# Half norms of a two-layer diffusion trunk: scale and shift move from VectorE to ScalarE, VectorE works in larger passes

## The chip, the core and the metric

The kernel runs on one core of a Trainium2 chip. The metric is the device time of one execution in microseconds; three runs of the kernel before gave a median of 2887.71 us (2882.85 to 2890.86). Engines are called PE (the matrix engine, TensorE), PEld (its weight loads), DVE (VectorE), ACT (ScalarE), POOL (GpSimd) and SP (the queue that starts the weight DMAs).

## The reference, cut to what matters

Two streams, 256 latent tokens (x) and 256 context tokens (h), go through two layers of the same shape: a half-step SwiGLU block, three token mixers side by side with gates, a second SwiGLU block. Each sub-layer is wrapped in RMS norms, and each norm ahead of a sub-layer is followed by an adaptive scale and shift:

```python
def rms_norm(x, g):
    xf = x.astype(jnp.float32)
    y = xf * lax.rsqrt(jnp.mean(xf * xf, axis=-1, keepdims=True) + EPS)
    return (y * g.astype(jnp.float32)).astype(x.dtype)

def modulate(x, shift, scale):
    return x * (1 + scale) + shift

def ffn_sublayer(t, shift, scale, gate, g_pre, g_post, w_in, w_out):
    y = swiglu(modulate(rms_norm(t, g_pre), shift, scale), w_in, w_out)
    return t + FFN_RES * gate * rms_norm(y, g_post)
```

All arithmetic is float32. D_MODEL is 1024, the FFN's inner width 2816.

## The kernel before, in words

**Layout.** Activations lie transposed: the 1024 channels are 8 chunks of 128 partitions, and the free axis holds the tokens, 256 latent ones and then 256 context ones. `x`, `work`, `xhi` and `xlo` are 128 x 8 x 512 tiles. A scale or a shift is one number for each channel and stream, so for one chunk and one stream it is a column of 128 numbers (`mods`); the inverse root `inv` is one number for each token, the same in all partitions and chunks.

**Products in three parts.** PE multiplies in a reduced format, so both operands are split in a high part and the rest. For a group of weights (128 x 1024, 512 KB, loaded into `raw`) ACT makes the high part `whi` (L1166) and DVE the rest `wlo` (L1474). PE then runs the group's first part, high and low activations by `whi` (L1934 and L1935, or L1998 and L2000 for products whose output is turned), and its second part, high activations by `wlo` (L1942, or L1995). There are two buffers of `whi` and `wlo`: the split of group k can begin only when PE has used group k-2, and group k's first part waits for `whi`, its second part for `wlo`. The activations' split is `xhi` and `xlo`; a first group waits for `xlo` chunk by chunk.

**Half norms.** In eight places the norm between two sub-layers is done for the 256 tokens of one stream alone, while PE multiplies for the other stream. Each engine runs such a norm as a generator that is advanced once for each group of the products beside it (`beside`): in slot k an engine first does its work for the products (the split of group k, and perhaps an output tile, L1279 and L1282), then the k-th piece of the norm. Pieces that find no group left follow one after another. Each engine works strictly in the order written. The products beside the eight norms are: the second stream's FFN output (12 groups; three norms, near 409, 1676 and 2050 us), values of the mixers (10 groups; two norms, near 444 and 2085 us), the mixers' output projection (8 groups, an output tile in each slot; one norm, near 1303 us) and the first groups of the next FFN for one stream (8 groups; two norms, near 1334 and 1710 us).

**The pieces of one half norm.** DVE: slot 1 refines the inverse root of the branch's output (Newton steps, L617, L630, L631 and L621); slots 2 and 3 add the residual in two batches of four chunks (L1651, L1654); slots 3 and 4 sum squares (L1661, L1682), which ACT made (L1323); slot 5 refines the second inverse root; slots 6 to 9 compute x times scale times inverse root, two chunks in each (`scaled`, L1633); slots 7 to 10 compute the low parts, two chunks in each (`normed_low`, L1643, which adds the shift once more and subtracts `xhi`). ACT: slot 5 makes the inverse root; slot 6 is empty; slots 7 to 10 add the shift and round to `xhi`, two chunks in each (`normed_high`, L1330). POOL adds the squares of the output tiles into `acc` (L1028).

Of the kernel before, what the change touches and what calls it, by code (L numbers as in the profile page):

```python
# [8 lines left out]
F32 = mybir.dt.float32  # L9
F32R = mybir.dt.float32r  # L10
ALU = mybir.AluOpType
ACT = mybir.ActivationFunctionType
AX_X = mybir.AxisListType.X

P = 128
D = 1024
KC = D // P
S = 256
# [27 lines left out]
BATCHES = 2  # L46
# [109 lines left out]
def make_plan():  # L156
# [14 lines left out]

    def half_norm(layer, post, pre, half):

        adds = {"stat": 2, "inv": 2, "gated": BATCHES, "x": BATCHES, "xsq": BATCHES, "xsum": 3, "scaled": KC,
                "xhi": KC, "xlo": KC}
        return add("norm", layer, post=post, pre=pre, tokens=S, span=(half * S, half * S + S), adds=adds, half=True)

    def last_products(layer, post, pre, **kw):
# [147 lines left out]
def build(nc, io, silu_rows, x_kept, out):  # L326
# [3 lines left out]
    with ExitStack() as ctx:  # L330
# [103 lines left out]
        def sem(name):  # L434
# [19 lines left out]
        first_shift = sem("first_shift")  # L454
        ada_dot = sem("ada_dot")
        done = {name: sem(f"{name}_done") for name in (
            "ghi", "glo", "gated", "xsq", "xsum", "sq", "acc", "stat", "inv", "x", "scaled", "xhi",
            "xlo", "rope", "m", "mhi", "mlo", "vk", "lsq", "lstat", "lln", "linv", "lvar", "lt", "lhi", "llo",
            "score", "bias", "exp", "prob", "turned", "pt", "pv", "yraw", "ysq", "yln", "yinv", "yfactor",
            "yscaled", "yturned", "yback", "yhi", "ylo", "ybhi", "yblo", "ln", "refined", "made")}  # L460
# [33 lines left out]
        def base(ph, name):  # L494
            return ph.at.get(name, 0)
# [5 lines left out]
        def batch(t, ph, b):  # L501

            return t[:, b * KC // BATCHES:(b + 1) * KC // BATCHES, ph.span]
# [119 lines left out]
        def newton(step, dve, count, bank_, cols, width):  # L623

            dst, v = inv[:, cols], tmp[:, 0, cols]
            newton_start(dve, count, bank_, cols, width, v)
            dve.wait_ge(done["refined"], count)

            dve.wait_ge(done["inv"], count)
            step(dve.tensor_tensor(v, v, dst, ALU.mult))  # L630
            step(dve.tensor_tensor(v, v, dst, ALU.mult))  # L631
            newton_end(step, dve, dst, v)
# [518 lines left out]
        def _(act):  # L1151
# [173 lines left out]
            def normed_high(ph, c):  # L1325

                l, sub = ph.pre
                act.wait_ge(done["scaled"], base(ph, "scaled") + c + 1)
                for s in streams(ph.span):
                    last = act.activation(xhi[:, c, sl(s)], work[:, c, sl(s)], ACT.Identity,  # L1330
                                          bias=mods[:, l, 3 * sub, c, s:s + 1])
                last.then_inc(done["xhi"], 1)

            def act_norm(ph):

                inverse(HALF_STAT, ph.span, D, base(ph, "stat") + 1)
                yield
                yield
                square(ph, 0)
                yield  # L1340
                square(ph, 1)
                yield
                inverse(HALF_STAT, ph.span, D, base(ph, "stat") + 2)
                yield
                yield
                for c in range(0, KC, 2):
                    normed_high(ph, c)
                    normed_high(ph, c + 1)
                    yield

            use_table(SILU)
# [114 lines left out]
        def _(dve):  # L1466
# [162 lines left out]
            def scaled(ph, c):  # L1629

                l, sub = ph.pre
                for s in streams(ph.span):
                    last = dve.scalar_tensor_tensor(work[:, c, sl(s)], x[:, c, sl(s)],  # L1633
                                                    mods[:, l, 3 * sub + 1, c, s:s + 1], inv[:, sl(s)],
                                                    ALU.mult, ALU.mult)
                last.then_inc(done["scaled"], 1)
# [11 lines left out]
            def residual_added(ph, b):  # L1648
# [5 lines left out]
                dve.tensor_tensor(batch(x, ph, b), batch(x, ph, b), batch(work, ph, b), ALU.add)\  # L1654
                   .then_inc(done["x"], 1)

            def squares_summed(ph, b):

                dve.wait_ge(done["xsq"], base(ph, "xsq") + b + 1)
                first, second = squares[:, 4 * b:4 * b + 2, :], squares[:, 4 * b + 2:4 * b + 4, :]  # L1660
                dve.tensor_tensor(first, first, second, ALU.add).then_inc(done["xsum"], 1)  # L1661
# [8 lines left out]
            def dve_norm(ph):  # L1670

                newton(step, dve, base(ph, "inv") + 1, HALF_STAT, ph.span, D)
                residual_ready(ph)
                yield
                residual_added(ph, 0)
                yield
                residual_added(ph, 1)
                squares_summed(ph, 0)
                yield
                squares_summed(ph, 1)  # L1680
                dve.wait_ge(done["xsum"], base(ph, "xsum") + 2)
                dve.tensor_tensor(squares[:, 0:2, :], squares[:, 0:2, :], squares[:, 4:6, :],  # L1682
                                  ALU.add).then_inc(done["xsum"], 1)
                yield
                newton(step, dve, base(ph, "inv") + 2, HALF_STAT, ph.span, D)
                yield
                for c in range(0, KC + 2, 2):
                    if c < KC:
                        scaled(ph, c)
                        scaled(ph, c + 1)  # L1690
                    if c:
                        normed_low(ph, c - 2)
                        normed_low(ph, c - 1)
                    yield

            spreads = 0

# [482 lines left out]
```

## Time and profile before

| | |
|---|---|
| median of three runs | 2887.71 us |
| the profiled execution's own time | 2884.27 us |
| its span, first to last instruction | 2882.2 us |
| PE busy | 2770.0 us, 96% |
| DVE busy | 1743.8 us, 61% |
| ACT busy | 1250.8 us, 43% |
| POOL busy | 249.1 us, 9% |
| granted TensorE clock, mean | 0.985 of full |

Busy times are unions over the span. A timeline row gives start and duration in us, engine, line, operation, output and inputs, shapes and how many instructions were merged; a bracket is idle time of the engine before it and what ended it. Consecutive instructions of DVE and of ACT overlap by some 0.1 us at their ends, so the pace is read from start to start.

### The profile page before, as it was taken

How to read it: one execution, taken by the hardware profiler on the slowest of the kernel's cores; microseconds unless marked ns; L12 is line 12 of the kernel's file. 1: busy time of each engine (PE TensorE's matmuls, PEld its weight loads, DVE VectorE, ACT ScalarE, POOL GpSimd, SP SyncE). 2: the span in 40 equal slices, each digit the busy share in tenths (PEclk: the TensorE clock that was granted, in tenths of full speed). 3: DMA queues.
4: the chain of work that ended last, by engine and by line, in shares of the span. 5: the costliest groups of instructions: out<-in, count | busy, mean ns of one | idle time of the engine just before them, and what ended most of it. 6: DMA issues, size and time to landing. Idle time of an engine off the chain costs nothing.

```text
span 2882.2 us, 42837 instructions
## 1 busy us (share of the span) xinstructions
PE 2770.0 (96%) x15754; PEld 2301.8 (80%) x15754; DVE 1743.8 (61%) x2907; ACT 1250.8 (43%) x2227; POOL 249.1 (9%) x342
## 2 busy tenths in 40 slices
PE   6999999999889999999999999999999899998997
PEld 4888898876656676788888898888988677878997
DVE  5677366656745444358676386773778765635764
ACT  2232355336545434445322363223553655555443
POOL 0010010111200000011000000000102120001000
PEclk8999999999999999999999999999999999999999
DMA  5555357331111121145455355553565221424654
GB/s 224 181 188 197 108 156 241 126 101 37 45 37 38 52 77 66 44 146 175 160 191 171 114 175 177 201 182 97 176 198 186 69 66 59 137 66 154 227 175 130
DMA packets 106643, 385.48 MB, mean 134 GB/s; under 512 B 12289, under 2 KB 14081, under 8 KB 104193
## 3 DMA queue, kind: packets, MB, share of 16 engines
q1 hardware_dynamic: 86370, 303.82, 32.6%
q0 software_dynamic: 20128, 79.70, 8.4%
q8 instruction: 94, 1.54, 0.2%
q14 instruction: 51, 0.42, 0.0%
HBM read 379.27 MB, written 4.20 MB: 133 GB/s over the span
## 4 chain that ended last, share of the span: by engine, by line
PE 85%; DVE 9%; ACT 2%; issue 2%; DMA 1%; POOL 0%; SPq 0%; DVEq 0%; POOLq 0%; ACTq 0%
PE ps L1934 23%; PE ps L1935 22%; PE ps L1942 22%; PE ps L879 3%; PE ps L917 3%; PE ps L896 3%; DVE wlo L1474 2%; PE ps L1998 1%; PE ps L2000 1%; PE ps L1995 1%; PE ps L869 1%; DVE mx L767 1%; PE ps L875 1%; DVE work L1633 1%; ACT prob L683 1%
## 5 line engine op out<-in xcount | busy, mean ns | idle before, releaser
L1474 DVE TENSOR_TENSOR wlo<-raw,whi 128x1024 fp32r<-128x1024 f32 x572 | 696.2, 1225 | 442.2 <-ACT whi L1166 441.4
L1934 PE MATMUL ps<-xhi,whi 128*128 128x512 f32 (+1 forms) x2432 | 827.2, 354 | 16.5 <-DVE xlo L1643 16.5
L1935 PE MATMUL ps<-xlo,whi 128*128 128x512 f32 (+1 forms) x2432 | 818.3, 351 | 0.0
L1166 ACT ACTIVATE whi<-raw 128x1024 fp32r<-128x1024 f32 x572 | 604.8, 1057 | 483.6 <-PE ps L1942 443.9
L1934 PEld LDWEIGHTS ps<-xhi,whi 128*128 128x128 f32 x2432 | 465.8, 192 | 85.8 <-DVE xlo L1643 18.8
L1935 PEld LDWEIGHTS ps<-xlo,whi 128*128 128x128 f32 x2432 | 466.7, 192 | 57.0
L1942 PE MATMUL ps<-xhi,wlo 128*128 128x512 f32 (+1 forms) x2432 | 507.4, 351 | 1.4 <-DVE wlo L1474 1.4
L1942 PEld LDWEIGHTS ps<-xhi,wlo 128*128 128x128 f32 x2432 | 401.8, 191 | 59.3 <-DVE wlo L1474 2.0
L1710 DVE SCALAR_TENSOR_TENSOR work<-ada,work 128x1024 f32<-128x1024 f32 x256 | 299.8, 1221 | 4.4 <-DMA ada<-in_ada_rows 4.4
L1934 PE MATMUL ps<-ghi,whi 128*128 128x256 f32 (+1 forms) x968 | 279.5, 314 | 1.9 <-ACT whi L1166 1.9
L1935 PE MATMUL ps<-glo,whi 128*128 128x256 f32 (+1 forms) x968 | 278.6, 314 | 0.0
L767 DVE TENSOR_REDUCE mx<-ps 128x2 f32<-128x1024 f32 (+1 forms) x120 | 125.2, 1045 | 241.3 <-PE ps L883 88.1
L1408 ACT ACTIVATE ghi<-tmp 128x512 f32 (+2 forms) x88 | 51.0, 580 | 343.0 <-DVE tmp L1793 343.0
L1934 PEld LDWEIGHTS ps<-ghi,whi 128*128 128x128 f32 x968 | 183.2, 189 | 15.2 <-issue 2.8
L1935 PEld LDWEIGHTS ps<-glo,whi 128*128 128x128 f32 x968 | 183.0, 189 | 12.1
L1942 PE MATMUL ps<-ghi,wlo 128*128 128x256 f32 (+1 forms) x968 | 168.4, 314 | 3.4 <-DVE wlo L1474 3.4
L1793 DVE TENSOR_TENSOR tmp<-tmp,ps 128x512 f32<-128x512 f32 (+1 forms) x88 | 54.6, 621 | 181.4 <-PE ps L1942 181.4
L1942 PEld LDWEIGHTS ps<-ghi,wlo 128*128 128x128 f32 x968 | 140.9, 188 | 16.2 <-DVE wlo L1474 4.1
L896 PE MATMUL ps<-ident,prob 128*128 128x128 f32 x640 | 107.0, 282 | 32.3 <-ACT ya L729 14.1
L896 PEld LDWEIGHTS ps<-ident,prob 128*128 128x128 f32 x640 | 72.4, 142 | 65.0 <-issue 32.1
L1048 POOL DMA_DIRECT2D ada<-in_ada_rows x128 | 68.6, 536 | 607.4 <-DVE work L1710 603.8
L683 ACT ACTIVATE prob<-ps,mx 128x512 f32<-128x512 f32 (+1 forms) x144 | 87.3, 612 | 76.6 <-DVE mx L767 73.5
(209 smaller groups left out, 3374.4 us busy)
## 6 DMA issues: line engine op xcount, KB each, us to landing
raw<-in_ffn_in SPq DMA_DIRECT2D x192, 512.0 KB, 4.8
ada<-in_ada_rows POOLq DMA_DIRECT2D x128, 512.0 KB, 4.4
raw<-in_merge SPq DMA_DIRECT2D x96, 512.0 KB, 3.7
raw<-in_ffn_out SPq DMA_DIRECT2D x88, 512.0 KB, 3.6
raw<-in_ffn_out SPq DMA_DIRECT2D x44, 384.0 KB, 3.2
raw<-in_v_a SPq DMA_DIRECT2D x32, 512.0 KB, 4.3
raw<-in_qk_a SPq DMA_DIRECT2D x32, 512.0 KB, 3.6
raw<-in_wo SPq DMA_DIRECT2D x24, 512.0 KB, 3.7
```

The source lines that it names most:

```text
L683: last = act.activation(prob(u)[:, n, 0:nk], ps[:, SCORE + 2 * e + n, 0:nk], ACT.Exp, bias=shift[:, e, n:n + 1], accum_out=sm[:, r, n:n + 1])
L767: largest = dve.tensor_reduce(mx[:, e, :], ps[:, SCORE + 2 * e:SCORE + 2 * e + 2, 0:nk], AX_X, ALU.max, negate=True)
L879: last = pe.matmul(o, q[half, b, cols], k[half, kb, ks], start=True, stop=not masked)
L896: last = pe.transpose(ps[:, TURN, cs], prob(u)[:, n, cs], ident[:, :])
L917: last = pe.matmul(ps[rows, OUT, to:to + P], a, w, start=kc == kc0, stop=kc == T // P - 1)
L1048: pool.dma_start(ada[:, slot, :], src).then_inc(ada_loaded[slot], 16)
L1166: act.activation(whi[:, g.ring(SPLIT), :], raw[:, g.ring(RAW), :], ACT.Copy).then_inc(hi_ready, 1)
L1474: dve.tensor_tensor(wlo[:, g.ring(SPLIT), :], raw[:, g.ring(RAW), :], whi[:, g.ring(SPLIT), :].bitcast(F32), ALU.subtract).then_inc(lo_rea ...
L1710: dve.scalar_tensor_tensor(products[:, s, :], ada[:, slot, :], 1.0, c_all[:, s * D:(s + 1) * D], ALU.mult, ALU.mult, accum_out=to).then_in ...
L1934: pe.matmul(o, w, hi[:, first + c, ph.span], start=start, stop=False)
L1935: pe.matmul(o, w, lo[:, first + c, ph.span], start=False, stop=False)
L1942: last = pe.matmul(ps[:, n.ring(BANKS), ph.span], wlo[:, s, col:col + P], hi[:, first + c, ph.span], start=False, stop=stop)
```

## The change

The generator pieces of the half norms change, on ACT and DVE alone. DVE multiplies x by the inverse root in two passes of four chunks (`normalized`, in slots 5 and 6); ACT applies scale and shift to each chunk in place (`modulated`) and rounds two chunks at once to `xhi` (`highs`), in slots 6, 7 and 8, the last with four chunks; DVE subtracts two chunks at once (`lows`), in slots 7, 8 and, twice, 9. A new counter, `modulated`, stands between ACT's two steps. The norms of full width are as before.

```diff
+            def modulated(ph, c):
+
+                l, sub = ph.pre
+                s = ph.span.start // S
+                act.wait_ge(done["scaled"], base(ph, "scaled") + c * BATCHES // KC + 1)
+                act.activation(work[:, c, ph.span], work[:, c, ph.span], ACT.Identity,
+                               bias=mods[:, l, 3 * sub, c, s:s + 1], scale=mods[:, l, 3 * sub + 1, c, s:s + 1])\
+                   .then_inc(done["modulated"], 1)
+
+            def highs(ph, c):
+
+                act.wait_ge(done["modulated"], base(ph, "modulated") + c + 2)
+                act.activation(xhi[:, c:c + 2, ph.span], work[:, c:c + 2, ph.span], ACT.Copy)\
+                   .then_inc(done["xhi"], 2)
+
...
                 inverse(HALF_STAT, ph.span, D, base(ph, "stat") + 2)
                 yield
-                yield
-                for c in range(0, KC, 2):
-                    normed_high(ph, c)
-                    normed_high(ph, c + 1)
+                for chunks in (range(2), range(2, 4), range(4, KC)):
+                    for c in chunks:
+                        modulated(ph, c)
+                        if c % 2:
+                            highs(ph, c - 1)
                     yield
...
+            def normalized(ph, b):
+
+                many = [P, KC // BATCHES, S]
+                dve.tensor_tensor(batch(work, ph, b), batch(x, ph, b),
+                                  inv[:, ph.span].unsqueeze(1).to_broadcast(many), ALU.mult).then_inc(done["scaled"], 1)
+
+            def lows(ph, c):
+
+                dve.wait_ge(done["xhi"], base(ph, "xhi") + c + 2)
+                dve.tensor_tensor(xlo[:, c:c + 2, ph.span], work[:, c:c + 2, ph.span],
+                                  xhi[:, c:c + 2, ph.span].bitcast(F32), ALU.subtract).then_inc(done["xlo"], 2)
+
...
                 newton(step, dve, base(ph, "inv") + 2, HALF_STAT, ph.span, D)
-                yield
-                for c in range(0, KC + 2, 2):
-                    if c < KC:
-                        scaled(ph, c)
-                        scaled(ph, c + 1)
-                    if c:
-                        normed_low(ph, c - 2)
-                        normed_low(ph, c - 1)
-                    yield
+                normalized(ph, 0)
+                yield
+                normalized(ph, 1)
+                yield
+                lows(ph, 0)
+                yield
+                lows(ph, 2)
+                yield
+                lows(ph, 4)
+                lows(ph, 6)
```

## Rows read from the trace of the kernel before

**Rows 1.** The page: busy time by engine, and shares of the chain by engine.

```profile
PE 2770.0 (96%) x15754; PEld 2301.8 (80%) x15754; DVE 1743.8 (61%) x2907; ACT 1250.8 (43%) x2227; POOL 249.1 (9%) x342
PE 85%; DVE 9%; ACT 2%; issue 2%; DMA 1%; POOL 0%; SPq 0%; DVEq 0%; POOLq 0%; ACTq 0%
```

**Rows 2.** One line's instructions: durations min/median/max in ns, first and last start.

```profile
L1651 DVE TENSOR_TENSOR work<-work,inv x16: 1210/1218/1759, 406.4 to 2085.9; 128x1024 f32<-128x1024 f32 x16
```

**Rows 3.** Timeline of PE, the norm near 409 us: part starts, groups 6 to 9.

```profile
421.29 1.12 PE L1942 MATMUL ps<-ghi,wlo 128*128 128x256 f32 x8
422.25 0.29 PE L1934 MATMUL ps<-ghi,whi 128*128 128x256 f32 x1
...
425.13 0.29 PE L1934 MATMUL ps<-ghi,whi 128*128 128x256 f32 x1
...
427.29 0.29 PE L1934 MATMUL ps<-ghi,whi 128*128 128x256 f32 x1
```

**Rows 4.** Timeline of DVE, the same norm, from the end of its refinement.

```profile
419.23 0.42 DVE L621 SCALAR_TENSOR_TENSOR inv<-tmp,inv 128x256 f32<-128x256 f32 x1
419.69 1.23 DVE L1474 TENSOR_TENSOR wlo<-raw,whi 128x1024 fp32r<-128x1024 f32 x1
420.84 1.36 DVE L1633 SCALAR_TENSOR_TENSOR work<-x,mods,inv 128x256 f32<-128x256 f32 x2
...
423.26 0.87 DVE L1633 SCALAR_TENSOR_TENSOR work<-x,mods,inv 128x256 f32<-128x256 f32 x2
```

**Rows 5.** Timeline of ACT, the same norm.

```profile
419.49 1.06 ACT L1166 ACTIVATE whi<-raw 128x1024 fp32r<-128x1024 f32 x1 [0.33 <-PE ps L1942]
420.45 0.37 ACT L1279 ACTIVATE tmp<-ps 128x256 f32<-128x256 f32 x1
420.72 0.47 ACT L1282 ACTIVATE work<-ps,mods 128x256 f32<-128x256 f32 x1
...
423.77 0.91 ACT L1330 ACTIVATE xhi<-work,mods 128x256 fp32r<-128x256 f32 x2
```

**Rows 6.** Timelines near 1361 us: ACT and DVE on a 128x512 tile.

```profile
1361.41 0.63 ACT L1408 ACTIVATE ghi<-tmp 128x512 fp32r<-128x512 f32 x1 [2.27 <-DVE tmp L1793]
...
1362.07 0.69 DVE L1799 TENSOR_TENSOR glo<-tmp,ghi 128x512 fp32r<-128x512 f32 x1 [0.70 <-ACT ghi L1408]
```

**Rows 7.** Timelines, norms near 444, 1303, 1334 us: split of group 6, PE's second part.

```profile
454.05 1.22 DVE L1474 TENSOR_TENSOR wlo<-raw,whi 128x1024 fp32r<-128x1024 f32 x1
455.99 1.07 PE L1995 MATMUL ps<-wlo,xhi 128*128 128x512 f32 x4
1313.90 0.74 POOL L1028 TENSOR_TENSOR acc<-acc,tmp 128x256 f32<-128x256 f32 x1 [3.99 <-ACT tmp L1279]
1314.09 1.64 DVE L1474 TENSOR_TENSOR wlo<-raw,whi 128x1024 fp32r<-128x1024 f32 x1
1316.28 1.12 PE L1942 MATMUL ps<-mhi,wlo 128*128 128x256 f32 x8
1345.08 1.23 DVE L1474 TENSOR_TENSOR wlo<-raw,whi 128x1024 fp32r<-128x1024 f32 x1
1346.92 1.12 PE L1942 MATMUL ps<-xhi,wlo 128*128 128x256 f32 x8
```

**Rows 8.** Waits of PE near 1310:1330, 1340:1358 and 1716:1733 us: total, times, longest.

```profile
PE ps L1934 <- DVE xlo L1643: 2.8, 2, 2.3
...
PE ps L1934 <- DVE xlo L1643: 1.5, 2, 0.8
...
PE ps L1934 <- DVE xlo L1643: 1.1, 2, 0.7
```

**Rows 9.** Windows: length, busy of PE, PEld, DVE, ACT, POOL; clock, DMA, GB/s.

```profile
1320.00:1332.00 12.00, 9.16 (x48) 8.38 (x47) 10.07 (x19) 5.46 (x10) 1.20 (x1) 0.72 0.35 117
1352.00:1360.00 8.00, 7.12 (x41) 6.62 (x42) 5.36 (x10) 5.08 (x7) 1.61 (x3) 0.79 0.62 222
1727.00:1731.00 4.00, 2.86 (x16) 2.06 (x15) 3.49 (x9) 3.30 (x6) 0.21 (x1) 1.00 0.46 138
```

More of the change, by code:

```diff
@@ L172, in half_norm @@
     def half_norm(layer, post, pre, half):
-        adds = {"stat": 2, "inv": 2, "gated": BATCHES, "x": BATCHES, "xsq": BATCHES, "xsum": 3, "scaled": KC,
-                "xhi": KC, "xlo": KC}
+        adds = {"stat": 2, "inv": 2, "gated": BATCHES, "x": BATCHES, "xsq": BATCHES, "xsum": 3,
+                "scaled": BATCHES, "modulated": KC, "xhi": KC, "xlo": KC}
         return add("norm", layer, post=post, pre=pre, tokens=S, span=(half * S, half * S + S), adds=adds, half=True)
@@ L456, in build @@
         done = {name: sem(f"{name}_done") for name in (
-            "ghi", "glo", "gated", "xsq", "xsum", "sq", "acc", "stat", "inv", "x", "scaled", "xhi",
+            "ghi", "glo", "gated", "xsq", "xsum", "sq", "acc", "stat", "inv", "x", "scaled", "modulated", "xhi",
             "xlo", "rope", "m", "mhi", "mlo", "vk", "lsq", "lstat", "lln", "linv", "lvar", "lt", "lhi", "llo",
```

## The prediction, made before the changed kernel ran

> **What bounds the kernel now.** I read the page first. PE is busy 96% of the span and has 85% of the chain that ended last; DVE has 9%, ACT 2% [rows 1]. So a microsecond that PE stands still is a microsecond of the whole, and work taken from DVE or ACT is worth only the waits of PE that it ends. The page's 61% and 43% for DVE and ACT are averages over stages and say nothing of a half norm. The residual is multiplied in two passes for each half norm and 16 times in all, so there are eight half norms [rows 2]. Then I read PE's waits around each of the eight. After the second inverse root PE waits on the norm's result in three of them alone: 2.8 us near 1323, 1.5 us near 1352, 1.1 us near 1728, 5.4 us in sum [rows 8]. These are the norms with 8 groups beside them, where slots 9 and 10 find no group. Around the first two the granted clock is below full, 0.72 on average over 12 us and 0.79 over 8 us, around the third it is 1.00 [rows 9]. PE was busy nearly all of the time at the lower level, 1.2 in place of 2.4 GHz, so the shares missing, 12 x 0.28 and 8 x 0.21, are the price: 3.4 and 1.7 us. In the other five norms PE has no wait from there on. So the change can win at most 5.4 + 5.1 = 10.5 us; what it can lose is read from the slack of the weight splits in slots 6 to 9.
>
> **The pieces and their prices.** DVE loses eight `scaled` and eight `normed_low` (a pair takes 0.87 us, 0.79 until the next can start, since DVE's instructions overlap by 0.08 [rows 4]), 6.3 us; it gains two `normalized`, nearest row the four-chunk multiply by the same broadcast, 1.22 us, 1.15 from start to start, up to 1.76 [rows 2, 4], and four `lows`, 0.69 us, nearest row the 128x512 subtraction [rows 6], 0.6 from start to start: 4.7 us. DVE does 1.6 us less, but earlier: a whole `normalized` now stands ahead of the split of group 6.
>
> ACT loses eight `normed_high`, two of which take 0.91 us (0.82 from start to start). It gains eight `modulated`, which no row shows. With a column as scale and one as shift, the nearest rows are 0.47 us (scale only, 128x256) and half of the pair of 0.91 (shift only) [rows 5]; bounds 0.37 us, the bare square of such a tile, and 0.6 us, the 128x512 copy. I take 0.41 from start to start. And it gains four `highs`, 0.63 us, 0.54 from start to start with ACT's overlap of 0.1 [rows 5, 6], each of which must wait until the second `modulated` has written (0.50 + 0.03 in place of 0.41). A pair of chunks costs 0.41 + 0.53 + 0.54 = 1.48 us instead of 0.82; a norm 2.6 us more. Nobody hides that by ACT's 57% idle: ACT's next act in each slot is a weight split that PE needs within one group's 2.88 us.
>
> **One FFN-output norm, slot by slot** (near 409, 1676, 2050 us). DVE's refinement ends at 419.65. `normalized` 0 takes 419.69 to 420.92, and the split of group 6 starts at 420.84 instead of 419.69 [rows 4], ending at 422.06. PE wanted it at 421.29 [rows 3]: wait 0.81 us, first part of group 7 due at 423.06 instead of 422.25.
> ACT in slot 6, empty before, now waits in order for `normalized` 0: `modulated` 420.95 and 421.36, `highs` 421.89, and only then the high split of group 7 at 422.43, which began at 419.49 before [rows 5]. It ends at 423.47: wait 0.46 us.
> From there ACT has no pause: split 0.97, output tile 0.68 (the starts at 419.49, 420.45 and the end of the tile's pair in rows 5), chunks 2 and 3 1.48, and the split of group 8 starts at 425.56, ends at 426.60; PE is due at 423.52 + 2.88 = 426.40: wait 0.25.
> Slot 8 holds four chunks, 2.96 us: split of group 9 starts at 426.53 + 2.96 = 429.49, ends at 430.53. Group 8 is the short third part of a tile (422.25 to 425.13 is a long group, 425.13 to 427.29 a short one of 2.16 [rows 3]), so PE is due at 426.65 + 2.16 = 428.81: wait 1.77. Then ACT has nothing more of the norm and catches up.
> Sum 3.3 us for each, 9.9 us for three. Nothing given back: these norms had no wait after slot 5.
>
> **Two value norms** (near 444, 2085 us), the same steps. The split of group 6 moves from 454.05 to 455.20, ends 456.42, PE wanted it at 455.99 [rows 7]: 0.48. The high split of group 7, by the same chain, 0.55. In slot 7 ACT carries two value tiles (0.95 us) instead of an output tile: 0.68. Slot 8: 1.2. Sum 2.9, twice 5.8 us.
>
> **The output-projection norm** (near 1303 us). The split of group 6 already took 1.64 us beside a POOL addition [rows 7]; now `normalized` takes that place and its stretch, and the split ends near 1316.9, PE wanted it at 1316.28: 0.6. Then 0.5 and 0.25 as above, the tile in each slot. Next comes the first group of the following product, which waits on `xlo`: chunks 2, 4 and 6 arrive behind ACT's slot 8 at 1323.3, 1324.3 and 1325.8, the last half microsecond of matmuls then ending at 1326.3. Before, without the half clock, that group would have ended near 1326.1, by its last `xlo`. With one more stretch by POOL +1.0 is the far end, +0.2 the near one; I take +0.6.
>
> One rule of the Trainium skill weighs on this. In the output-projection norm a DVE instruction with two operands in SBUF ran 1.64 us beside a POOL addition, 1.23 alone [rows 4, 7]. "SBUF — State Buffer", section "Who interferes with whom", says that a DVE instruction with two SBUF inputs contends with a GpSimd instruction that reads SBUF; by it `normalized` and `lows` are no safer than what they replace, and the trace agrees. A stretch of 0.4 us in each of the four norms with output tiles would make the sum 1.6 us longer.
>
> **The two norms beside the next FFN** (near 1334, 1710 us) have no output tiles. The split of group 6: 1345.08 + 1.15 + 1.22 = 1347.45 against 1346.92 [rows 7], 0.5 (0.24 in the other); then 0.45; ACT, without tiles, is in time for group 8; chunk 2 of the first following group waits 0.95, chunk 4 0.1, chunk 6 0.75, 2.5 to 2.8 us in all, against 2.3 us by which that group was stretched before. +0.3 each, 0.6 in all. The freed slot buys nothing here: what was late behind DVE's slot 10 is now late behind ACT's slot 8.
>
> **Sum:** 9.9 + 5.8 + 0.6 + 0.6 = 16.9 us. The clock I leave as it was: waits of the same size end in the same places. The profiled execution took 2884.27 us, 3.4 less than the median of the three runs; the mean of all four executions is 2886.4. 2886.4 + 16.9 = 2903.
>
> **The rivals.**
> *ACT's idle hides it (faster).* Place: ACT's slots 6 to 8. If ACT's passes were at their low bound and the chain through `normalized` 0 cost nothing, DVE's lighter slots would end the waits of rows 8 and the half clock behind them: 10.5 us less, 2876. It decides from the point where the high split of group 7 ends before 422.2. For it: DVE is full in slots 6 to 9 (2.72 us of work in slots of 2.88), ACT idle 43% to 57%. Against: ACT's in-order wait for `normalized` 0, which ends at 420.92 and leaves 0.3 us for 2.5 us of work. 8%. The Trainium skill's "Perfetto Trace Analysis", section "Optimizing Scalar/DVE Operations", speaks for this rival: with DVE saturated, moving work to Scalar may help, and larger operations raise throughput; by that rule the time would be 2876. The same section says that where the engines cause bubbles elsewhere, smaller instructions finish sooner, which is my case.
> *It cancels (within 0.3%).* Only the first two waits of each norm stand: 3 x 1.27 + 2 x 1.03 + 1.1 + 1.0 + 0.7 = 8.7 us, and a half-clock stretch or two goes (5.1), or ACT's low bound empties the waits of slot 8: +0 to +8, 2886 to 2894. 24%.
> *The clock falls at the new waits.* A new wait of 1.8 us stands in three norms and of 1.2 in two; if each brings a stretch at 1.2 GHz that costs 1.7 us, as the one near 1352 did, it is five times 1.7, 8.5 us more: 2912. For it: the clock fell around waits of this size. Against: around 1.1 us in two pieces it stayed full [rows 8, 9]. 10%.
>
> **Chances.** Forecast, 2896.5 to 2909: 58%. Rivals 8, 24 and 10%. Slower by over 0.3% (8.7 us, about what a measurement of this kernel can tell from no change) is 68%, within 0.3% 24%, faster 8%. The forecast's own range is 2896.5 to 2909; for 8 in 10 it reaches down into the cancelling case and up into the clock case: 2885 to 2914.
>
> **What would show it.** In the changed profile: PE waits on `wlo` (L1474) for group 6 in all eight norms, 0.2 to 0.9 us; PE waits on `whi` (L1166) for groups 7 to 9, together 2.5 us in FFN-output norms; ACT without a pause between slots 6 and 9; `modulated` at 0.5 us, `normalized` at 1.2. I am wrong if PE has no such waits, if the waits on `xlo` vanish in the three norms with 8 groups, or if ACT's pair of chunks takes under 1.1 us.

## The result and the profile after

The changed kernel takes 2905.21 us in the median of five runs (2903.29 to 2911.32), beside 2887.71 for five runs of the kernel before (2882.74 to 2890.86): a ratio of 1.0064, 95% interval 1.0047 to 1.0081. It is slower, by more than the 0.3% that the prediction counts as no change. The forecast was 2903, within 2885 to 2914.

The page after, busy times by engine and the chain by engine (they answer to [rows 1]):

```profile
span 2901.6 us, 42845 instructions
...
PE 2770.0 (95%) x15754; PEld 2296.6 (79%) x15754; DVE 1733.4 (60%) x2827; ACT 1272.4 (44%) x2259; POOL 253.3 (9%) x342
...
PE 82%; DVE 9%; ACT 5%; issue 2%; DMA 1%; POOL 1%; SPq 0%; DVEq 0%; ACTq 0%; POOLq 0%
```

PE does the same work in the same busy time and stands still for longer; ACT's share of the chain rose from 2% to 5%, though it is busy for only 22 us more. PE's waits over the whole program, largest first (engine and line, who ended the wait: us in total, times, longest):

```profile
PE ps L1963 <- ACT whi L1166: 11.3, 11, 2.0
...
PE ps L1971 <- DVE wlo L1490: 9.2, 10, 1.1
...
PE ps L1963 <- DVE xlo L1682: 5.6, 6, 1.0
...
PE ps L2027 <- ACT whi L1166: 4.8, 6, 1.3
```

L1963 and L2027 are the first parts of a group (L1934 and L1998 before), L1971 the second part (L1942), L1682 the new `lows`. For `whi` PE waited 2.5 us in the kernel before, none of it in a half norm; now it is 11.3 + 4.8 = 16.1. The row of before:

```profile
PE ps L1934 <- ACT whi L1166: 2.5, 3, 1.9
```

The first FFN-output norm, near 409 us. PE's timeline of the kernel before at the start of this stretch, second part of group 5:

```profile
418.52 0.87 PE L1942 MATMUL ps<-ghi,wlo 128*128 128x256 f32 x6
```

and of the kernel after, the same part and the part starts of [rows 3]:

```profile
417.20 0.87 PE L1971 MATMUL ps<-ghi,wlo 128*128 128x256 f32 x6
...
420.78 1.21 PE L1971 MATMUL ps<-ghi,wlo 128*128 128x256 f32 x8 [0.65 <-DVE wlo L1490]
...
422.53 0.36 PE L1963 MATMUL ps<-ghi,whi 128*128 128x256 f32 x1 [0.54 <-ACT whi L1166]
...
425.72 0.39 PE L1963 MATMUL ps<-ghi,whi 128*128 128x256 f32 x1
...
430.17 0.36 PE L1963 MATMUL ps<-ghi,whi 128*128 128x256 f32 x1 [2.04 <-ACT whi L1166]
```

The stretch begins 1.32 us earlier than before. Second part of group 6: 0.51 earlier, so 0.81 lost. First part of group 7: 0.28 later, 1.60 lost. Group 8: 0.59 later, 1.91 lost. Group 9: 2.88 later, 4.20 lost. DVE and ACT over the same stretch (they answer to [rows 4, 5]):

```profile
417.90 0.43 DVE L621 SCALAR_TENSOR_TENSOR inv<-tmp,inv 128x256 f32<-128x256 f32 x1
418.36 1.23 DVE L1676 TENSOR_TENSOR work<-x,inv 128x1024 f32<-128x1024 f32 x1
419.51 1.22 DVE L1490 TENSOR_TENSOR wlo<-raw,whi 128x1024 fp32r<-128x1024 f32 x1
420.64 1.22 DVE L1676 TENSOR_TENSOR work<-x,inv 128x1024 f32<-128x1024 f32 x1
422.42 1.23 DVE L1490 TENSOR_TENSOR wlo<-raw,whi 128x1024 fp32r<-128x1024 f32 x1 [0.56 <-ACT whi L1166]
423.56 1.23 DVE L1682 TENSOR_TENSOR xlo<-work,xhi 128x512 fp32r<-128x512 f32 x1
```

```profile
419.62 1.09 ACT L1339 ACTIVATE work<-work,mods 128x256 f32<-128x256 f32 x2 [1.79 <-DVE work L1676]
420.81 0.63 ACT L1346 ACTIVATE xhi<-work 128x512 fp32r<-128x512 f32 x1
421.35 1.04 ACT L1166 ACTIVATE whi<-raw 128x1024 fp32r<-128x1024 f32 x1
422.29 0.36 ACT L1279 ACTIVATE tmp<-ps 128x256 f32<-128x256 f32 x1
422.56 0.47 ACT L1282 ACTIVATE work<-ps,mods 128x256 f32<-128x256 f32 x1
422.91 1.08 ACT L1339 ACTIVATE work<-work,mods 128x256 f32<-128x256 f32 x2
424.09 0.63 ACT L1346 ACTIVATE xhi<-work 128x512 fp32r<-128x512 f32 x1
424.63 1.04 ACT L1166 ACTIVATE whi<-raw 128x1024 fp32r<-128x1024 f32 x1
425.57 1.08 ACT L1339 ACTIVATE work<-work,mods 128x256 f32<-128x256 f32 x2
426.75 0.63 ACT L1346 ACTIVATE xhi<-work 128x512 fp32r<-128x512 f32 x1
427.29 1.07 ACT L1339 ACTIVATE work<-work,mods 128x256 f32<-128x256 f32 x2
428.45 0.63 ACT L1346 ACTIVATE xhi<-work 128x512 fp32r<-128x512 f32 x1
428.99 1.99 ACT L1166 ACTIVATE whi<-raw 128x1024 fp32r<-128x1024 f32 x2
```

What the reader is to see: ACT sits idle for 1.79 us in front of its first new instruction, with the high split of group 7 behind it in the queue; and from 419.62 it has no pause longer than 0.1 us until the two splits at 428.99, which it makes back to back because both are due by then. ACT is 44% busy over the program and busy all but 0.4 us of these 11.

I measured all eight norms like this, by the starts of PE's second part of one and the same group in both traces: the first just ahead of the norm's second half, the other where the waits have ended. Clock parts come from the share of time at 1.2 GHz.

| norm (near, us, in the kernel before) | foretold | measured step | of it clock | without clock |
|---|---|---|---|---|
| 409, FFN output | 3.3 | 4.2 | 0 | 4.2 |
| 444, values | 2.9 | 3.9 | 0 | 3.9 |
| 1303, projection | 0.6 | 0.5 | -1.7 | 2.2 |
| 1334, next FFN | 0.3 | 0.1 | -1.7 | 1.8 |
| 1676, FFN output | 3.3 | 5.7 | +1.7 | 4.0 |
| 1710, next FFN | 0.3 | 1.3 | 0 | 1.3 |
| 2050, FFN output | 3.3 | 6.1 | +1.7 | 4.4 |
| 2085, values | 2.9 | 3.9 | 0 | 3.9 |
| sum | 16.9 | 25.7 | 0 | 25.7 |

The rest of the program gave back 6.3 us in this one execution: 1.3 ahead of the first norm and 5.1 in the last layer's attention and FFN, whose code did not change. The clock column rests on these windows of the kernel after (columns as in [rows 9], to which the first two answer):

```profile
1330.00:1342.00 12.00, 10.01 (x65) 9.29 (x64) 8.92 (x11) 7.17 (x12) 1.60 (x2) 0.86 0.40 121
1359.00:1367.00 8.00, 6.18 (x47) 5.52 (x46) 5.24 (x6) 7.13 (x11) 1.61 (x3) 1.00 0.63 217
1703.00:1712.00 9.00, 6.96 (x46) 6.79 (x46) 4.70 (x5) 5.01 (x8) 1.16 (x1) 0.81 0.52 158
2086.00:2095.00 9.00, 7.56 (x51) 7.59 (x52) 5.33 (x5) 3.94 (x6) 1.15 (x1) 0.81 0.45 157
```

The projection norm's stretch at the lower clock is half as long as before (12 x 0.14 = 1.7 us lost, not 3.4), that of the norm behind it is gone (before 1.7), and two have come after FFN-output norms (9 x 0.19 = 1.7 each). Over the eight norms the sum is zero.

### The profile page after: what moved, and what is told of

Read it like the earlier page. It is cut to its first block, busy times and chain, and to the rows that moved or that the text cites. A ratio compares the mean times of both kernels' runs of the same rounds, so it can differ in the third digit from the quotient of the medians.

```text
span 2901.6 us, 42845 instructions
## 1 busy us (share of the span) xinstructions
PE 2770.0 (95%) x15754; PEld 2296.6 (79%) x15754; DVE 1733.4 (60%) x2827; ACT 1272.4 (44%) x2259; POOL 253.3 (9%) x342
## 4 chain that ended last, share of the span: by engine, by line
PE 82%; DVE 9%; ACT 5%; issue 2%; DMA 1%; POOL 1%; SPq 0%; DVEq 0%; ACTq 0%; POOLq 0%
PE ps L1963 22%; PE ps L1964 22%; PE ps L1971 22%; PE ps L917 3%; PE ps L879 3%; PE ps L896 2%; DVE wlo L1490 2%; ACT whi L1166 1%; PE ps L869 1%; PE ps L2027 1%; PE ps L2029 1%; PE ps L2024 1%; ACT work L1339 1%; DVE mx L767 1%; PE ps L875 1%
## 5 line engine op out<-in xcount | busy, mean ns | idle before, releaser
L1963 PE MATMUL ps<-xhi,whi 128*128 128x512 f32 (+1 forms) x2432 | 824.3, 353 | 17.8 <-DVE xlo L1659 11.0
L1963 PEld LDWEIGHTS ps<-xhi,whi 128*128 128x128 f32 x2432 | 464.0, 191 | 87.2 <-DVE xlo L1659 12.0
L1971 PE MATMUL ps<-xhi,wlo 128*128 128x512 f32 (+1 forms) x2432 | 507.0, 351 | 2.1 <-DVE wlo L1490 2.0
L1971 PEld LDWEIGHTS ps<-xhi,wlo 128*128 128x128 f32 x2432 | 400.9, 191 | 60.8 <-DVE wlo L1490 3.1
L1963 PE MATMUL ps<-ghi,whi 128*128 128x256 f32 (+1 forms) x968 | 281.0, 315 | 9.8 <-ACT whi L1166 9.6
L1963 PEld LDWEIGHTS ps<-ghi,whi 128*128 128x128 f32 x968 | 183.8, 190 | 24.8 <-issue 11.6
L1971 PE MATMUL ps<-ghi,wlo 128*128 128x256 f32 (+1 forms) x968 | 169.2, 315 | 5.7 <-DVE wlo L1490 5.7
L1971 PEld LDWEIGHTS ps<-ghi,wlo 128*128 128x128 f32 x968 | 141.8, 190 | 19.2 <-DVE wlo L1490 7.0
L1028 POOL TENSOR_TENSOR acc<-acc,tmp 128x256 f32<-128x256 f32 (+1 forms) x68 | 68.9, 1014 | 612.6 <-ACT tmp L1279 452.5
```

Source lines behind the costliest of these rows:

```text
L1028: pool.tensor_tensor(acc[:, cols], acc[:, cols], tmp[:, number, cols], ALU.add)\
L1963: pe.matmul(o, w, hi[:, first + c, ph.span], start=start, stop=False)
L1971: last = pe.matmul(ps[:, n.ring(BANKS), ph.span], wlo[:, s, col:col + P], hi[:, first + c, ph.span], start=False, stop=stop)
```

## The experiments

Theory A: a queue worked in order is late for PE's next group for two reasons, DVE's large pass ahead of group 6's low split, and ACT's new work ahead of the high splits of groups 7 to 9 (where it stands, and how long it takes). Rivals: ACT's load alone (B), group 6's delay as the root of all (C), the slot with four chunks alone (D), placement alone (E). The experiments were compared with two sets of 29 runs of the kernel before, with medians of 2885.01 (first four experiments) and 2885.32 us (last four); the changed kernel's ratio is that to its five runs. "Norms" is the sum of the eight steps in the profiled execution, measured as above, "rest" what the remainder of the program differs by.

The last three columns take the clock apart. A run with a mean granted clock c over a span T has lost about (1 - c) x T to the lower clock, as the prediction reckons it from [rows 9]; in the kernel before that is 43.5 and 44.5 us on average. "Norms, no clock" leaves this out of the eight steps by the stretches at 1.2 GHz in each trace, an estimate: 1.7 us for a stretch of 3.4. "Runs, clock" is the difference of that loss between the mean of all timed runs and the mean of the 29, "runs, no clock" the difference of the mean times that is left, known to 1 to 2 us.

| kernel | median us | ratio, 95% interval | norms | rest | norms, no clock | runs, clock | runs, no clock |
|---|---|---|---|---|---|---|---|
| changed kernel | 2905.21 | 1.0064 (1.0047 to 1.0081) | +25.7 | -6.3 | +25.7 | -7 | +27 |
| ACT one slot later | 2891.62 | 1.0021 (1.0011 to 1.0032) | +7.1 | +3.1 | +8.8 | -1.6 | +7.2 |
| last slot split | 2901.10 | 1.0050 (1.0033 to 1.0066) | +15.1 | +1.1 | +18.5 | -4.3 | +18.9 |
| all one slot later | 2890.71 | 1.0011 (0.9999 to 1.0023) | +9.0 | +7.2 | +3.9 | -0.6 | +5.0 |
| old pieces, new slots | 2882.84 | 0.9997 (0.9984 to 1.0010) | +4.4 | -4.2 | +7.8 | -9.6 | +9.1 |
| two-chunk passes | 2903.07 | 1.0056 (1.0041 to 1.0070) | +18.5 | +5.0 | +21.9 | -4.4 | +22.1 |
| no rounding pass | 2886.73 | 1.0000 (0.9992 to 1.0009) | -0.4 | -2.6 | +3.0 | -2.3 | +2.7 |
| new pieces in short norms | 2889.49 | 1.0012 (1.0003 to 1.0021) | +2.2 | -6.0 | +5.6 | -3.1 | +6.0 |
| mixed chunks | 2881.40 | 0.9982 (0.9973 to 0.9991) | -3.5 | +4.5 | -0.1 | -4.0 | -0.6 |

Without the clock the profiled norms and the timed runs agree within 2 us for all nine kernels: what the change does to the waits is in both, and what the clock adds or gives back is separate from it.

**ACT one slot later.** The same instructions, ACT's slot 6 empty again and its last four chunks in two slots.

```diff
                 inverse(HALF_STAT, ph.span, D, base(ph, "stat") + 2)
                 yield
-                for chunks in (range(2), range(2, 4), range(4, KC)):
+                yield
+                for chunks in (range(2), range(2, 4), range(4, 6), range(6, KC)):
...
                 lows(ph, 4)
+                yield
                 lows(ph, 6)
```

> The changed kernel with ACT's pieces where they stood before: slot 6 empty, two chunks in each of slots 7 to 10, and DVE's four subtractions in slots 7, 8, 9 and 10; DVE's two large passes stay in slots 5 and 6. Theory A (ACT's place: it waits in order for DVE's first pass ahead of the high split of group 7, and slot 8 holds four chunks): PE's waits on the high split go in the five norms with 10 and 12 groups (some 2.6 us in each of three, 2.4 in each of two, 12.7 us), PE's waits for group 6's low split stay (3.5 us in all eight), the three norms with 8 groups gain about 1 us at most: 2890 to 2893 us. Rival B (ACT's load: its passes cost 3 us more per norm wherever they stand): 2902 to 2906. Rival C (everything follows from group 6's late low split): 2902 to 2906, with the waits on the high split still there.

2891.6 us. PE's waits in the first FFN-output norm, all that is left there (416 to 436 us):

```profile
PE ps L1973 <- DVE wlo L1491: 0.7, 1, 0.7
```

There is not one wait on a high split in the five long norms (those with 10 and 12 groups beside them), with ACT's load unchanged. That fells rival B (load wherever it stands) and rival C (group 6 as the root): group 6 is as late as in the changed kernel and nothing follows from it. 13.6 us of the 20 lost are ACT's place, its early start and its last slot with four chunks together; with the clock taken off it is 20 of 27. What remains is the waits for group 6, in the five long norms and the projection norm, and the three short norms (those with 8 groups).

**Last slot split.** ACT starts in slot 6 as in the changed kernel, but has two chunks in slot 8 and two in slot 9.

```diff
-                for chunks in (range(2), range(2, 4), range(4, KC)):
+                for chunks in (range(2), range(2, 4), range(4, 6), range(6, KC)):
...
                 lows(ph, 4)
+                yield
                 lows(ph, 6)
```

> The changed kernel with ACT's last slot split in two: ACT in slots 6, 7, 8 and 9, two chunks each; DVE's subtractions in slots 7, 8, 9 and 10. Theory A: the wait for group 9's high split falls from 2.0 to about 0.4 us in three norms and from 1.3 to about 0 in two, 7 us; the waits for groups 6 and 7 stay: 2897 to 2900 us. Rival B (load): 2902 to 2906. Rival D (only the four chunks in one slot matter): 2890 or less, the waits for group 7 gone too.

2901.1 us, 1 us over the expected range and 4 under the changed kernel; the intervals of the two overlap, and the traces tell them apart. PE's timeline in the first FFN-output norm:

```profile
421.42 1.22 PE L1972 MATMUL ps<-ghi,wlo 128*128 128x256 f32 x8 [0.66 <-DVE wlo L1490]
423.18 0.36 PE L1964 MATMUL ps<-ghi,whi 128*128 128x256 f32 x1 [0.54 <-ACT whi L1166]
429.12 0.36 PE L1964 MATMUL ps<-ghi,whi 128*128 128x256 f32 x1 [0.34 <-ACT whi L1166]
```

Group 9's wait is 0.34 in place of 2.04, group 7's is what it was. So the slot with four chunks is 1.7 of the 4.2 us. The rest, with rival D fallen, is the early start, of DVE's pass (0.81 us) and of ACT's pieces.

**All one slot later.** DVE's two passes also move, behind the low split of group 6.

```diff
                 newton(step, dve, base(ph, "inv") + 2, HALF_STAT, ph.span, D)
+                yield
                 normalized(ph, 0)
                 yield
                 normalized(ph, 1)
-                yield
                 lows(ph, 0)
```

> As the kernel with ACT's pieces in slots 7 to 10, and DVE's two large passes one slot later as well, in slots 6 and 7, behind the low split of group 6. Theory A: no wait for group 6's low split, none on high splits but 0.3 us or so in the norms with output tiles; in the three norms with 8 groups the last chunks come 1 to 1.5 us later than in the kernel before, since ACT's pair of chunks takes 1.7 us where it took 0.8: 2888 to 2892 us, some 1 to 3 us under the kernel whose DVE passes stand in 5 and 6. Rival B (load): still over 2900.

2890.7 us. In the long norms no view lists a wait of PE; their steps are 0.3 to 0.5 us each. The three short norms pay: PE waits 3.8, 2.5 and 2.6 us for `xlo` there, where it was 2.8, 1.5 and 1.1 [rows 8], and their steps are 1.0, 2.1 and 3.6 us, of which the clock is 0, 1.7 and 3.4. The new arithmetic is all but free where groups stand beside it, and it is longer than the old one where they don't.

**Old pieces, new slots.** The kernel before, its single-chunk instructions put where the change puts its own.

```diff
                 newton(step, dve, base(ph, "inv") + 2, HALF_STAT, ph.span, D)
-                yield
-                for c in range(0, KC + 2, 2):
...
+                for c in range(4):
+                    scaled(ph, c)
+                yield
+                for c in range(4, KC):
+                    scaled(ph, c)
+                yield
+                for chunks in (range(2), range(2, 4), range(4, KC)):
+                    for c in chunks:
+                        normed_low(ph, c)
+                    yield
```

(ACT likewise: `normed_high` for chunks 0 and 1, 2 and 3, and 4 to 7 in slots 6 to 8.)

> The arithmetic of the kernel before (DVE multiplies by scale and inverse root chunk by chunk and adds the shift in the subtraction, ACT adds the shift) in the slots of the changed kernel: DVE four chunks in slot 5 and four in slot 6, subtractions 2, 2 and 4 in slots 7 to 9; ACT 2, 2 and 4 chunks in slots 6 to 8. Theory A in its two halves: the low split of group 6 is late by DVE's 1.6 us ahead of it (1.0 to 1.4 us in each of five norms), but ACT gets its first chunks after 0.5 us instead of 1.2 and four chunks take 1.6 us instead of 3.4, so no wait on a high split: 2891 to 2895 us. If the slots alone were the cause (rival E): 2902 to 2906. If the load alone were (rival B): 2887.

2882.8 us, no different from the kernel before: a miss, 8 us under the lower end of what I expected. The mechanism is there: in the first FFN-output norm PE waits 1.1 us for group 6's low split and never for a high one.

```profile
418.15 0.91 ACT L1330 ACTIVATE xhi<-work,mods 128x256 fp32r<-128x256 f32 x2 [1.05 <-DVE work L1632]
418.97 1.04 ACT L1166 ACTIVATE whi<-raw 128x1024 fp32r<-128x1024 f32 x1
...
422.77 1.69 ACT L1330 ACTIVATE xhi<-work,mods 128x256 fp32r<-128x256 f32 x4
425.02 1.06 ACT L1166 ACTIVATE whi<-raw 128x1024 fp32r<-128x1024 f32 x1 [0.56 <-PE ps L1942]
```

Four chunks take ACT 1.69 us, not 3.4, and it waits for PE again behind them. The long norms' steps are 1.1 to 1.7 us, 7.1 in sum (forecast: 1.0 to 1.4 each). I had left out what the short norms get (-1.4, -1.1 and -0.2 us, of which the clock is 1.7 in each of the first two), and the rest of the program was 4.2 us shorter in this execution. The timed runs show where the cost went: nine of the 12 had a granted clock of 0.988 to 0.990, where the kernel before has 0.985 on average. The clock gave back 9.6 us, and without it this kernel is 9.1 us slower, within the 6 to 10 that I expected. So the delays are real and the time that hid them is the clock's; why this kernel kept the higher clock longer is open. Rival E (slots alone, 2902 to 2906) is out either way: in the same slots the changed kernel lost 27 us without the clock, and the difference is its longer ACT work.

**Two-chunk passes.** The changed kernel with `normalized` over two chunks, one pass in slot 5 and three in slot 6.

```diff
-                many = [P, KC // BATCHES, S]
-                dve.tensor_tensor(batch(work, ph, b), batch(x, ph, b),
+                many = [P, 2, S]
+                dve.tensor_tensor(work[:, 2 * b:2 * b + 2, ph.span], x[:, 2 * b:2 * b + 2, ph.span],
...
-                normalized(ph, 1)
+                for b in range(1, KC // 2):
+                    normalized(ph, b)
```

> The changed kernel with DVE's multiplication by the inverse root in passes of two chunks: one in slot 5, ahead of the low split of group 6, three in slot 6. The slots of ACT stay. Theory A: what stands ahead of that split falls from 1.15 to 0.6 us, so PE's waits for group 6's low split fall from 3.5 us in all eight norms to under 1, and ACT gets its first chunk 0.54 us sooner; the wait for the high split of group 7 follows the same shift and stays near 0.5, group 9's 2.0 and 1.3 stay: some 4 us less than the changed kernel, 2899 to 2902. Rival (the first pass doesn't matter, ACT's own time does): no change, 2903 to 2906.

2903.1 us: 1 over the expected range and within the changed kernel's interval, so the timing does not tell. The trace does: group 6 is 0.3 us late in place of 0.8 to 1.2 in the FFN-output norms and no longer late in the value norms; their steps are 0.5 us shorter each where the clock is the same. ACT's waits are as before:

```profile
421.50 0.36 PE L1964 MATMUL ps<-ghi,whi 128*128 128x256 f32 x1 [0.55 <-ACT whi L1166]
429.14 0.36 PE L1964 MATMUL ps<-ghi,whi 128*128 128x256 f32 x1 [2.02 <-ACT whi L1166]
```

**No rounding pass.** ACT's pair of chunks without its second step. This kernel leaves the scale and the shift out of the low parts, so it is a measurement and no replacement; DVE's subtraction takes as long as before (684 ns).

```diff
-                act.activation(work[:, c, ph.span], work[:, c, ph.span], ACT.Identity,
+                act.activation(xhi[:, c, ph.span], work[:, c, ph.span], ACT.Identity,
                                bias=mods[:, l, 3 * sub, c, s:s + 1], scale=mods[:, l, 3 * sub + 1, c, s:s + 1])\
-                   .then_inc(done["modulated"], 1)
+                   .then_inc(done["xhi"], 1)
...
                         modulated(ph, c)
-                        if c % 2:
-                            highs(ph, c - 1)
```

> The changed kernel without ACT's second step: the scale-and-shift instruction writes xhi itself, rounded, and there is no pass of two chunks behind it; this leaves the scale and the shift out of the low part (DVE subtracts xhi from the unscaled product), which takes DVE the same time. A pair of chunks costs ACT about 1.0 us in place of 1.72, in unchanged slots. Theory A (a slot's ACT work must fit ahead of its next split): no wait for the high split of group 7, 0.3 to 0.5 us left of 2.0 for group 9, the low split of group 6 late as before, the last chunks 1 to 1.5 us sooner in the three short norms: 15 to 19 us less than the changed kernel, 2884 to 2890. Rival (placement alone, one slot too early): 2898 or more, group 7 still late by 0.5 us because ACT waits for DVE's pass.

2886.7 us, as fast as the kernel before, in the changed kernel's slots. PE in the first FFN-output norm:

```profile
419.40 1.22 PE L1969 MATMUL ps<-ghi,wlo 128*128 128x256 f32 x8 [0.66 <-DVE wlo L1488]
425.91 0.36 PE L1961 MATMUL ps<-ghi,whi 128*128 128x256 f32 x1 [0.21 <-ACT whi L1166]
```

The second step, `highs` with its wait, is what makes the slots overflow: 0.72 us for each pair, and without it 18 of the 20 us are gone (24 of 27 without the clock). With the first experiment this settles the cause as place and length together. Take either away and the waits on high splits go, but for 0.2 us in each FFN-output norm here.

**New pieces in short norms.** The change in the three norms with 8 groups alone.

```diff
                 inverse(HALF_STAT, ph.span, D, base(ph, "stat") + 2)
                 yield
+                if not short(ph):
+                    yield
+                    for c in range(0, KC, 2):
+                        normed_high(ph, c)
+                        normed_high(ph, c + 1)
+                        yield
+                    return
...
```

(DVE likewise: its pieces of the kernel before where the norm isn't short.)

> The changed kernel's pieces in the three norms with 8 groups beside them alone, the kernel before's in the other five. Theory A: the five norms are as before, the three others each 1.3 to 2.2 us longer, less or more 1.7 for each stretch at half clock that comes or goes: 2886 to 2891. If the freed slot helped anywhere, it would be here: rival, 2875 to 2882.

2889.5 us. The five long norms' steps are 0.0 us, the short ones' 0.8, 0.2 and 1.3, the first two with 1.7 us of clock given back each. The freed slot wins nothing where it was freed.

**Mixed chunks.** What the experiments point to: DVE is full in the short norms, ACT, where it has no tile, has about 1.9 us beside its split in each of slots 7 and 8 (2.88 less 0.95), one new pair's worth. So in the short norms half of the chunks go the new way, one slot later than the change has them.

```diff
+                if short(ph):
+                    normalized(ph, 0)
+                    yield
+                    for c in (4, 6):
+                        scaled(ph, c)
+                        scaled(ph, c + 1)
+                        lows(ph, c - 4)
+                        yield
+                    for c in range(4, KC):
+                        normed_low(ph, c)
+                    return
...
```

(This is DVE's part. ACT makes scale, shift and rounding of chunks 0 to 3 in slots 7 and 8, and `normed_high` of chunks 4 to 7 in slots 8 and 9.)

> The kernel before, but in the three norms with 8 groups the first four chunks go the new way (one DVE pass in slot 6, ACT's scale and shift in slots 7 and 8, two subtractions of two chunks) and the last four the old way (DVE's scale in slots 7 and 8, ACT's shift in slots 8 and 9, single subtractions). DVE, which is full there, does 0.85 us less per norm, ACT has room for its 0.9 us more per pair. Theory A: the last xlo comes 0.1 us sooner in the projection norm and 0.5 us in the two others, no new wait on a split: 2883 to 2886, which these runs can't tell from the kernel before; the trace can. Rival (ACT's passes delay the following splits here too): over 2888, with waits on high splits in the trace.

2881.4 us, a ratio of 0.9982 (0.9973 to 0.9991) to the kernel before: small, its interval under 1, the fastest of all, and 1.6 us under the expected range. PE's waits in the short norm near 1719 us:

```profile
PE ps L1993 <- DVE xlo L1702: 1.2, 1, 1.2
```

One wait of 1.2 us where there were two of 1.1 in sum, with slower matmuls behind each [rows 8]; by the starts of the parts the step is -0.3 us, not quite the expected 0.5. The steps of the two others are -1.7 and -1.5, and in both the stretch at 1.2 GHz is 3.4 us shorter, 1.7 us of time: without the clock the three steps sum to -0.1. The 11 timed runs say the same, 4.0 us of their 4.5 us gain in the mean is the clock's, and -0.6 is left, less than its own uncertainty of 1.3. So the moved work costs nothing here and by itself wins nothing that can be told from zero; what was won is clock.

## Why the prediction was right

It named the direction, the place and the mechanism. The waits it named are in the trace but for two: beside the next FFN, group 6's second part is 0.2 us late in both norms (foretold 0.5 and 0.24), and no view lists a wait there. That the time came out 2 us from the forecast is in part luck, as the point on the sum says. Step by step:

- *The low split of group 6 is late by one DVE pass.* Foretold 0.81 us of loss in the FFN-output norm, measured 0.81 (0.80 and 1.19 in the two later ones). `normalized` took 1.22 us as its nearest row. Right.
- *ACT waits in order for the first pass, group 7's high split behind it.* Foretold 0.46, measured 0.79. Right in kind; of the 0.33 missing, 0.24 is the next point, and 0.09 that PE's first matmul starts 0.14 us behind the end of the split, not 0.05.
- *A pair of chunks costs ACT 1.48 us.* It costs 1.72: `modulated` with a column for scale and one for shift took 0.59 us, near the far bound I had given it and not the row with one column that I took, and 0.5 from start to start in place of 0.41; after the wait for its write `highs` begins 0.1 us later, not 0.03. This is the mis-sized term. Slot 8 holds two pairs, so group 9's loss is 2.29 and not 1.77; over the four groups of an FFN-output norm it makes 4.2 of 3.3, over a value norm 3.9 of 2.9.
- *The projection norm.* PE's wait for group 7 was foretold as 0.5, for `whi`; it is 1.12, and it is a wait for an output tile:

```profile
1323.83 1.22 PE L1971 MATMUL ps<-mhi,wlo 128*128 128x256 f32 x8 [0.51 <-DVE wlo L1490]
1326.17 0.36 PE L1963 MATMUL ps<-mhi,whi 128*128 128x256 f32 x1 [1.12 <-ACT work L1282]
...
1331.17 0.39 PE L1963 MATMUL ps<-xhi,whi 128*128 128x256 f32 x1 [1.03 <-DVE xlo L1682]
...
1333.61 0.39 PE L1963 MATMUL ps<-xhi,whi 128*128 128x256 f32 x1 [0.97 <-DVE xlo L1682]
```

  There each group is a tile of its own in one of two banks, so group 7 needs not only its split but ACT's copy of tile 5 out of the bank, which ends 0.64 us behind the split in the same slot. The prediction counted the tile as work on ACT and missed that PE waits for it. But this wait does not set the norm's loss: PE stands still again for `xlo`, twice, so a sooner group 7 would only have waited longer there. What ends last is `lows` for chunks 6 and 7, at 1333.55, behind ACT's slot 8. Less the 6.89 us by which the stretch begins later, that is 1326.7 where the prediction had 1325.8, and four pairs at 0.24 us more make it. Without clock this norm lost 2.2 us, not 0.6; 0.9 of the 1.6 is accounted for so, the rest is open.
- *The two norms beside the next FFN.* +1.8 and +1.3 without clock, foretold 0.3 each. The last `lows` stands behind four pairs of chunks, each 0.24 us longer than foretold: 1.0 us, which is all of the second norm's excess and most of the first's.
- *`normalized` and `lows` beside POOL.* The 0.4 us in each of four norms, named beside the sum, did not come for `normalized`: it took 1.64 us once, in the projection norm, where the sum has it, and 1.21 to 1.23 in the other 15. `lows` took 1.22 to 1.23 in place of 0.68 to 0.69 in eight of 32, all in the four norms with output tiles, and no wait in an FFN-output norm ends with one.
- *The clock stays as it was.* In the norms it did in the sum, 5.1 us lost before and after, but not place by place; over the program it did not, as the next point says. The rival "the clock falls at the new waits" was true in two of five long norms.
- *Sum.* 16.9 us foretold for the norms, 25.7 measured in the profiled execution; the medians of five runs each lie 17.5 us apart, 20 against the later runs. The norms lost half again as much as the terms say. The forecast of 2903 was nearer than its terms because the rest of the program, where nothing was changed, got shorter: by 6.3 us in the profiled execution, whose granted clock was 0.988 in place of 0.985. The timed runs say the same: four of the five have 0.988, the kernel before 0.985 on average, and (1 - c) x T is some 7 us less. Without that the changed kernel is 27 us slower, 10 more than the terms, and the time would have been near 2912. The prediction has no term for it; that the two misses cancel is luck.
- *The rival "ACT's idle hides it".* It fell, for the reason given: the engine is idle 56% of the program and not in the ten microseconds that count. As for the Trainium skill's advice in "Perfetto Trace Analysis", section "Optimizing Scalar/DVE Operations", to offload to Scalar when DVE is saturated: the page says that it may make sense. In the mixed kernel, where the moved work fits ahead of the next split, it cost nothing and won nothing but clock (norms -0.1 us without it); in the changed kernel, where it does not fit, it cost 25.7. The same section's advice to break instructions up where they cause bubbles held: two-chunk passes took 0.5 us off each long norm.

## What to carry to other kernels

An engine that works in order between deadlines has as much free time as stands ahead of its next deadline, and its busy share of the program says nothing of that: sum a slot's instructions start to start, and compare with the slot. Before moving work one slot earlier, look at what the receiving engine must wait for there and at what is queued behind that wait. And price an instruction at the far bound when its nearest row lacks one of its operands; here the second column cost 0.09 us in each of 64 instructions, and four pairs of them stood one behind the other ahead of the last wait of a norm.

## What the runs showed of the hardware

- An idle time that a row shows in front of a matmul is less than what is lost. In the FFN-output norm the brackets sum to 3.3 us, the starts of the same parts shift by 4.2. A matmul is drawn 0.28 us long and the next starts 0.12 later when nothing holds it, so each pause hides 0.16 us in the end of the matmul ahead of it, and group 8's further 0.31 us has no bracket at all. Starts of the same instruction in two traces give the loss.
- ACT with scale and shift both as columns, 128x256 in float32, SBUF to SBUF: 583 to 603 ns in 64 instances; with the shift alone 489 to 512 ns.

```profile
L1339 ACT ACTIVATE work<-work,mods x64: 583/588/603, 419.6 to 2125.5; 128x256 f32<-128x256 f32 x64
L1346 ACT ACTIVATE xhi<-work x32: 629/632/635, 420.8 to 2126.1; 128x512 fp32r<-128x512 f32 x32
```

- Stretches at 1.2 GHz move with every shift of the program's timing, in stages that are the same in all kernels: between the second and the third half norm, mostly attention, the eight experiments and the changed kernel stood at 0.0 to +7.3 us against the kernel before, behind the eighth at -7.0 to +2.8, and 29 runs of one kernel spread over 2878.5 to 2893.5 us. Differences under some 5 us can't be read off a single profiled execution's span; the steps of the stages that changed can. With (1 - c) x T taken off each of those 29 runs they lie within 5.4 us in place of 15.0, although c is given to 0.001 only, which is 2.9 us; most of the spread of one kernel is the clock's.
